# Gate and up products of three feed-forwards in Strassen's seven-product form

## What is computed

```python
h = rms_norm(x, norm_ffn_pre_g[l])
f = (jax.nn.silu(h @ w_gate[l]) * (h @ w_up[l])) @ w_down[l]          # first block
...
def swiglu(h, w_gu, w_down):                                          # second block, twice
    gu = h @ w_gu
    gate, up = jnp.split(gu, 2, axis=-1)
    return (jax.nn.silu(gate) * up) @ w_down
x = x + 0.5 * swiglu(rmsnorm(x, ffn1_norm[l]), ffn1_w_gu[l], ffn1_w_down[l])
```

## Time and profile before

| | us |
|---|---|
| median of 3 runs | 1953.12 (1953.09 to 1955.43) |
| the profiled execution's own time | 1954.23 |
| its span, first to last instruction | 1952.4 |
| PE busy | 1933.2 (99%) |
| DVE busy | 1005.9 (52%) |
| ACT busy | 753.4 (39%) |
| POOL busy | 237.6 (12%) |

### The profile page before, as it was taken

The page is one execution under the profiler, slowest core; times in us unless marked ns, Lnnn a source line. Parts: engine busy times, 40 slices in busy tenths (PEclk is TensorE's granted clock), DMA queues, the critical chain, the costliest instruction groups (busy, mean ns, idle before and its releaser), DMA issues.

```text
span 1952.4 us, 22990 instructions
## 1 busy us (share of the span) xinstructions
PE 1933.2 (99%) x9154; PEld 1576.6 (81%) x9154; DVE 1005.9 (52%) x1525; ACT 753.4 (39%) x1165; POOL 237.6 (12%) x240
## 2 busy tenths in 40 slices
PE   9999999999999999999999999999999999999998
PEld 7777788878888888788888888888887788888887
DVE  6677535373334345633343467887754443334335
ACT  6344534453223234432322356655643343223224
POOL 5210001201011011010100112222010011011010
PEclk9999999999999999999999999999999999999999
DMA  6122133433333323333333232222232233333323
GB/s 175 56 65 65 55 102 103 119 98 97 98 97 97 97 84 110 97 98 97 97 97 98 78 106 65 66 65 65 87 91 61 78 95 97 97 98 97 97 60 103
DMA packets 340763, 176.25 MB, mean 90 GB/s; under 512 B 6481, under 2 KB 339378, under 8 KB 340658
## 3 DMA queue, kind: packets, MB, share of 16 engines
q1 hardware_dynamic: 340658, 174.79, 30.6%
HBM read 172.67 MB, written 2.10 MB: 90 GB/s over the span
## 4 chain that ended last, share of the span: by engine, by line
PE 94%; DVE 3%; ACT 2%; issue 1%; DMA 1%; SPq 0%; POOL 0%; ACTq 0%; DVEq 0%
PE ps L1101 28%; PE ps L1105 28%; PE ps L1103 28%; PE ps L1161 1%; PE ps L1141 1%; PE ps L1150 1%; PE ps L1245 1%; PE ps L1114 1%; PE ps L1263 1%; PE ps L1124 1%; PE ps L1200 1%; PE ps L1131 0%; DVE WL L1555 0%; PE ps L1175 0%; DMA TS<-in_x 0%
## 5 line engine op out<-in xcount | busy, mean ns | idle before, releaser
L1101 PE MATMUL ps<-HH,WH 128*128 128x512 f32 x1728 | 688.3, 398 | 1.1 <-ACT HH L1316 1.1
L1105 PE MATMUL ps<-HL,WH 128*128 128x512 f32 x1728 | 674.1, 390 | 0.8 <-DVE HL L1576 0.8
L1103 PE MATMUL ps<-HH,WL 128*128 128x512 f32 x1728 | 673.6, 390 | 0.8 <-DVE WL L1555 0.8
L1555 DVE TENSOR_TENSOR WL<-RAW,WH 128x1024 fp32r<-128x1024 f32 (+3 forms) x335 | 400.6, 1198 | 530.2 <-ACT WH L1306 530.0
L1306 ACT ACTIVATE WH<-RAW 128x1024 fp32r<-128x1024 f32 (+3 forms) x335 | 337.6, 1010 | 520.9 <-PE ps L1105 517.8
L1101 PEld LDWEIGHTS ps<-HH,WH 128*128 128x128 f32 x1728 | 324.7, 188 | 78.1 <-issue 9.7
L1103 PEld LDWEIGHTS ps<-HH,WL 128*128 128x128 f32 x1728 | 324.9, 188 | 72.6 <-issue 5.5
L1105 PEld LDWEIGHTS ps<-HL,WH 128*128 128x128 f32 x1728 | 324.6, 188 | 71.4 <-DVE HL L1576 2.1
L1101 PE MATMUL ps<-GH,WH 128*128 128x512 f32 x688 | 269.2, 391 | 0.0
L1105 PE MATMUL ps<-GL,WH 128*128 128x512 f32 x688 | 268.0, 389 | 0.0
L1103 PE MATMUL ps<-GH,WL 128*128 128x512 f32 x688 | 267.7, 389 | 0.0
(11 more groups left out here) (203 smaller groups left out, 1555.0 us busy)
## 6 DMA issues: line engine op xcount, KB each, us to landing
RAW<-in_ffn_w_gu SPq DMA_DIRECT2D x88, 512.0 KB, 3.8
RAW<-in_w_in SPq DMA_DIRECT2D x67, 512.0 KB, 3.8
RAW<-in_ffn_w_down SPq DMA_DIRECT2D x32, 512.0 KB, 4.0
RAW<-in_w_gate SPq DMA_DIRECT2D x22, 512.0 KB, 3.7
RAW<-in_w_up SPq DMA_DIRECT2D x22, 512.0 KB, 3.7
RAW<-in_w_out SPq DMA_DIRECT2D x16, 512.0 KB, 4.1
RAW<-in_mem_w_kv SPq DMA_DIRECT2D x16, 512.0 KB, 3.9
RAW<-in_w_down SPq DMA_DIRECT2D x16, 512.0 KB, 3.9
```

What stands on the lines that cost most here:

```text
L1101: e.matmul(bk, wh, xh, start=k == 0, stop=False)
L1103: e.matmul(bk, wl, xh, start=False, stop=False)
L1105: last = e.matmul(bk, wh, xl, start=False, stop=k == kt - 1)
L1555: e.tensor_tensor(at.weight(n, "L"), m["RAW"][:, n % NRAW, 0:kt, :], at.weight(n, "H").bitcast(F32), ALU.subtract).then_inc(*sg.inc("lo", n))
```

## The change

From the fifth tile of the first third on, tiles are no longer made one by one but in pairs of two neighbouring tiles of 128 outputs (`pair`), first the pair's gate, then its up. With the outputs in two halves (tile f and f+1), the 1024 inputs in two halves (chunks 0 to 3 and 4 to 7) and the tokens in two halves (0 to 255 and 256 to 511), the product is a 2 x 2 by 2 x 2 block product, made with seven block products of 128 outputs, 512 inputs and 256 tokens instead of eight (`MIXED`, `product`): 7 x 4 x 3 = 84 matmuls of 256 columns in place of 48 of 512. The first four tiles of each feed-forward (`PLAIN`) stay as they were. Per feed-forward 9 gate pairs and 9 up pairs are made in the new way, 54 in all.

The sums of weights are made by POOL from the raw blocks (`combine_weights`, sums 1 to 4 of 128 x 512, tiles `S`); four of the seven products use a sum, three a half of a raw block. ACT and DVE split each of the seven in parts of 128 x 512 as before. The split places now count in halves, six in all (`HALVES_OF_RING`), so ACT's copy for product j waits for product j-6, and sits in the list behind it and behind the sums that follow it.

The sums of inputs need the normalised input itself: `normal` (DVE, x times gain times R, 8 tiles), `mix` (POOL, four sums of 128 x 256 for each of 4 chunk pairs), `mix_split` (ACT and DVE, into `NH`/`NL`), all during the plain tiles; and `place` (ACT and DVE) writes the normalised input itself over `HH`/`HL` once the last plain product has read them.

The seven results are added with the banks (U for a tile of their sums): ACT copies product 2's bank to U (`sum_one`, `s1`); DVE adds (`sum_one` u2, `sum_two` u3 and c22, `sum_three` c21, `sum_four` c12), each 128 x 256 from PSUM. Products 5 and 6 go on in the banks of products 2 and 1: product 5 (`"a", "21"`) waits for ACT's copy `s1`, and product 6 (`"c", "22"`) for DVE's c22. Silu is then on ACT in three pieces (`corner`, `silu_mixed`), gate by up on DVE (`corner`) and on POOL (`gate_mixed`, one of 128 x 512 and one of 128 x 256), in place of `gate_r` and `gate_up`.

The normalised tiles, `NH` and `NL` lie in memory that the attention's buffers and the masks have at other times, so the level masks and the constants `reset` and `AT` are made on POOL during the down products of the second feed-forward (`LATE`) and no longer at the start. The weight blocks that come by DMA are the same in number and size; of a pair the second comes first, and a raw buffer is free once its splits and sums are done.

The core of the diff:

```diff
+HALVES_OF_RING = 2 * NSPL
+PLAIN = 4
+MIXED = (("b", 2), ("c", 0), ("a", "11"), ("e", 1), ("d", 3), ("a", "21"), ("c", "22"))
...
+    def weigh_pair(self, key, name, c0):
+
+        n, r = len(self.weights), len(self.raws)
+        self.raws += [(name, 0, KD, c0 + P), (name, 0, KD, c0)]
+        self.weights += [("sum", key, 2), ("sum", key, 1), ("half", r + 1, 0), ("sum", key, 3), ("half", r, 1), ("half", r + 1, 1),
+                         ("sum", key, 4)]
+        self.pair_raws[key] = (r + 1, r)
+        self.raw_index += [None] * 7
+        self.needs += [r + 1] * 7
+        self.spent += [r] * 4 + [r + 1] * 2 + [r + 2]
+        self.raw_done[r] = (("lo", n + 4), ("comb", (key, 3)))
+        self.raw_done[r + 1] = (("lo", n + 2), ("lo", n + 5), ("comb", (key, 4)))
+        for _ in range(7):
+            self.offsets.append(self.offsets[-1] + 1)
...
+    def combine_to(self, key, j):
+
+        for i in range(self.combined.get(key, 0) + 1, j + 1):
+            self.tiles.take(("S", key, i))
+            self.step("combine_weights", key, i)
+            self.combined[key] = i
...
+    def ahead(self, n):
+
+        i = self.n_split
+        while i < self.total and self.known.offsets[i + 1] - HALVES_OF_RING <= self.known.offsets[n]:
+            i += 1
+        self.split_to(i)
...
+    def mix(self, gen, c, gcol):
+
+        if c < 4:
+            self.normal(gen, c, gcol)
+            self.normal(gen, c + 4, gcol)
+            for a in range(2):
+                self.tiles.take(("mix", gen, c, a))
+            self.step("mix", gen, c)
+        if c:
+            for a in range(2):
+                self.step("mix_split", gen, c - 1, a, self.mixed_free)
+                self.tiles.give(("mix", gen, c - 1, a), ("op_lo", ("T", gen, c - 1, a)))
+
+    def place(self, gen, c):
+
+        free = (("mm", len(self.weights) - 1),)
+        for a in range(2):
+            self.step("place", gen, c, a, free)
+            self.tiles.give(("N", gen, c + 4 * a), ("op_lo", ("B", gen, c, a)), ("mixed", (gen, c, 3)))
+
+    def pair(self, gen, G, f, up, name, c0, pending):
+
+        key = (G, f, up)
...
+        for i, (b, op) in enumerate(MIXED):
+            if i < 5:
+                self.bank(("pr", key, b))
+            self.step("product", gen, key, i, n + i)
+            if i < 2 and pending:
+                self.split_tile(*pending.pop(0))
+            elif i == 2:
+                self.tiles.take(("u", key))
+                self.step("sum_one", key, n)
+                self.banks.give(("pr", key, "b"), ("part_sum", ("u2", key)))
+            elif i == 3:
+                self.tiles.take(("w", key) if up else tb)
+                self.step("sum_two", key, n)
+                self.banks.give(("pr", key, "e"), ("part_sum", ("u3", key)))
+            elif i == 4:
+                self.step("sum_three", key, n)
+                self.banks.give(("pr", key, "d"), ("part_sum", ("c21", key)))
+                if up:
+                    self.step("gate_mixed", key, 1)
+                    self.tiles.give(("w", key), ("gm", (key, 1)))
+                else:
+                    self.step("silu_mixed", key, 1)
+            elif i == 5:
+                if not up:
+                    self.tiles.take(ta)
+                self.step("corner", key, n)
+                self.banks.give(("pr", key, "a"), ("part_sum" if up else "gate_act", ("c11", key)))
+            elif i == 6:
+                self.step("sum_four", key, n)
+                self.banks.give(("pr", key, "c"), ("part_sum", ("c12", key)))
+                if up:
+                    self.step("gate_mixed", key, 0)
+                    self.tiles.give(("u", key), ("gm", (key, 0)))
+                else:
+                    self.step("silu_mixed", key, 0)
+                    self.tiles.give(("u", key), ("part_sum", ("c12", key)))
+            self.ahead(n + i + 1)
+        return ("mm", n + 6)
...
+                if n or f >= PLAIN:
+                    if f % 2 == 0:
+                        self.pair(gen, G, f, 0, gate, g0 + (f0 + f) * P, pending)
+                        done = self.pair(gen, G, f, 1, up, u0 + (f0 + f) * P, pending)
+                        for a in range(2):
+                            pending.append((("gt", (G, f + a)), ("gm", ((G, f, 1), a)), "G", G, f + a, (("part_sum", ("c11", (G, f, 1))),)))
+                    continue
...
+                if f < PLAIN - 1:
+                    self.mix(gen, f, gcol)
+                else:
+                    self.mix(gen, f, gcol)
+                    self.mix(gen, f + 1, gcol)
+                    for c in range(4):
+                        self.place(gen, c)
+                    self.tiles.give(("R", ("n", gen)), ("N", (gen, 7)), ("gr", key))
+            while pending:
+                self.split_tile(*pending.pop(0))
...
+    def product(gen, key, i, n):
+        b, op = MIXED[i]
+        bk = at.bank(("pr", key, b))[:, 0:256]
+        wh, wl = at.weight(n, "H"), at.weight(n, "L")
+        if i < 5:
+            wait_all(at.bank_free(("pr", key, b)))
+        elif i == 5:
+            g.wait_ge(*sg.at("gate_act", ("s1", key)))
+        else:
+            g.wait_ge(*sg.at("part_sum", ("c22", key)))
+        for c in range(4):
+            ready = ("B" if i in (2, 5, 6) else "T", gen, c, 0 if op in ("11", 0, 1) else 1)
+            xh, xl = at.mixed(op, "H", c), at.mixed(op, "L", c)
+            g.wait_ge(*sg.at("hi", n))
+            g.wait_ge(*sg.at("op_hi", ready))
+            e.matmul(bk, wh[:, c, :], xh, start=i < 5 and c == 0, stop=False, skip_group_check=i >= 5)
+            g.wait_ge(*sg.at("lo", n))
+            e.matmul(bk, wl[:, c, :], xh, start=False, stop=False, skip_group_check=i >= 5)
+            g.wait_ge(*sg.at("op_lo", ready))
+            o = e.matmul(bk, wh[:, c, :], xl, start=False, stop=c == 3, skip_group_check=i >= 5)
+        o.then_inc(*sg.inc("mm", n))
 
...
+        kind, a, b, *_ = plan.weights[n]
+        if kind == "sum":
-            g.wait_ge(*sg.at("mm", n - NSPL))
-        e.activation(at.weight(n, "H"), m["RAW"][:, n % NRAW, 0:kt, :], ACT.Copy).then_inc(*sg.inc("hi", n))
+        else:
+            for i in plan.owners[n]:
+                g.wait_ge(*sg.at("mm", i))
+        e.activation(at.weight(n, "H"), at.raw(n), ACT.Copy).then_inc(*sg.inc("hi", n))
...
+    def sum_one(key, n):
+        g.wait_ge(*sg.at("mm", n + 2))
+        wait_all(at.tile_free(("u", key)))
+        e.activation(at.tile(("u", key))[:, 0:256], at.bank(("pr", key, "a"))[:, 0:256], ACT.Copy).then_inc(*sg.inc("gate_act", ("s1", key)))
...
+    def sum_one(key, n):
+        u = at.tile(("u", key))
+        g.wait_ge(*sg.at("gate_act", ("s1", key)))
+        g.wait_ge(*sg.at("mm", n))
+        e.tensor_tensor(u[:, 256:512], at.bank(("pr", key, "b"))[:, 0:256], u[:, 0:256], ALU.add).then_inc(*sg.inc("part_sum", ("u2", key)))
...
+    def sum_two(key, n):
+        u, home = at.tile(("u", key)), mixed_b(key)
+        g.wait_ge(*sg.at("part_sum", ("u2", key)))
+        g.wait_ge(*sg.at("mm", n + 3))
+        e.tensor_tensor(u[:, 0:256], at.bank(("pr", key, "e"))[:, 0:256], u[:, 256:512], ALU.add).then_inc(*sg.inc("part_sum", ("u3", key)))
+        g.wait_ge(*sg.at("part_sum", ("u3", key)))
+        wait_all(at.tile_free(home))
+        e.tensor_tensor(at.tile(home)[:, 256:512], at.bank(("pr", key, "c"))[:, 0:256], u[:, 0:256], ALU.add).then_inc(
+            *sg.inc("part_sum", ("c22", key)))
...
+    def combine_weights(key, j):
+        ra, rb = plan.pair_raws[key]
+        a, b = m["RAW"][:, ra % NRAW, :, :], m["RAW"][:, rb % NRAW, :, :]
+        out = at.raw_sum(key, j)
+        x, y, op = {1: (b[:, 0:4, :], b[:, 4:8, :], ALU.add), 2: (at.raw_sum(key, 1), a[:, 0:4, :], ALU.subtract),
+                    3: (a[:, 0:4, :], b[:, 0:4, :], ALU.subtract), 4: (a[:, 4:8, :], at.raw_sum(key, 2), ALU.subtract)}[j]
+        g.wait_ge(*sg.at(f"d_raw{rb % NRAW}", rb))
+        g.wait_ge(*sg.at(f"d_raw{ra % NRAW}", ra))
+        if j in (2, 4):
+            g.wait_ge(*sg.at("comb", (key, j // 2)))
+        wait_all(at.tile_free(("S", key, j)))
+        e.tensor_tensor(out, x, y, op).then_inc(*sg.inc("comb", (key, j)))
+
+    def mix(gen, c):
+        a, b = at.tile(("N", gen, c)), at.tile(("N", gen, c + 4))
+        u, v = at.tile(("mix", gen, c, 0)), at.tile(("mix", gen, c, 1))
+        g.wait_ge(*sg.at("N", (gen, c)))
+        g.wait_ge(*sg.at("N", (gen, c + 4)))
+        for i in range(2):
+            wait_all(at.tile_free(("mix", gen, c, i)))
+        e.tensor_tensor(u[:, 0:256], a[:, 256:512], a[:, 0:256], ALU.subtract).then_inc(*sg.inc("mixed", (gen, c, 0)))
+        e.tensor_tensor(u[:, 256:512], b[:, 256:512], a[:, 256:512], ALU.subtract).then_inc(*sg.inc("mixed", (gen, c, 2)))
+        g.wait_ge(*sg.at("mixed", (gen, c, 0)))
+        e.tensor_tensor(v[:, 0:256], b[:, 256:512], u[:, 0:256], ALU.subtract).then_inc(*sg.inc("mixed", (gen, c, 1)))
+        g.wait_ge(*sg.at("mixed", (gen, c, 1)))
```

(9 more changed lines are left out.)

265 lines of the change are left out of this document (199 added, 66 removed).

## The result

| us | before | after |
|---|---|---|
| median of 4 runs each | 1953.11 (1952.75 to 1955.43) | 2111.20 (2109.91 to 2112.27) |
| ratio | | 1.0805, 95% interval 1.0792 to 1.0817 |
| span of the profiled execution | 1952.4 | 2108.7 |

What follows compares the result with a forecast made beforehand. PE was taken as the bound, busy 1933.2 of 1952.4 us. PE's saving, POOL's chain and the starts, -44 + 76 + 24 = +56 us on 1954.2, gave 2010 us, with its own range 1985 to 2040 and an overall range of 1940 to 2050.

Steps and rivals of the forecast that it cites:

- PE's saving, 44 us: PE's matmuls in the new pairs: 10.08 us in place of 10.89, 0.81 saved in each of 54 pairs.
- Rival 4: PE's 256-column matmuls go at half the 512 pace, 0.1134 us each, saving 73 us: 1981 us; chance 0.05.
- The chain on POOL, 18 x 4.2 = 76 us: Gate pairs behind an up pair: POOL's late sums delay `s1` and c22, PE stalls 4.2 us, 18 times.
- DVE and POOL exclude each other: Of two operations with SBUF inputs the second waits for the first; 23.2 us of such work in 20.16 us.
- Rival 2: Gate pairs and starts: POOL's chain without blocking, 18 x 2.5 and 3 x 7.2 us: 1977 us; chance 0.17.
- the walk without blocking: Gate pair behind an up pair, nothing blocking: `s1` 1.6 us late, c22 0.9 more, together 2.5 us.
- The starts, 3 x 8 = 24 us: Where each feed-forward's new form starts, PE waits for the last mixed chunk and `place`: 8 us, three times.
- the other normals, sums and splits of inputs lie beside 43.6 us of plain matmuls: Input preparation during the plain tiles costs nothing; if late, it would add to the start.
- `place` was put at 4.4 us of DVE: At each start, eight `place` pieces on DVE take 0.42 and 0.69 us in turn.
- Rival 3, the clock: After stalls PE gets 1.2 GHz for 3.4 us, costing at most 18 x 1.7 = 31 us: 2041; chance 0.12.
- Rival 1, slack: The POOL chain in gate pairs has slack, stalls small or none: 1910 to 1935 us, up to 1949; chance 0.21.

Runs made afterwards that it cites:

- e16_nosums6: Changed kernel with six plain tiles, `place` by halves, hidden tile's splits later and each weight sum replaced by one fill (values left out): 1934.5 us.
- e1_sum3: Changed kernel with POOL making sum 3 of the next gate pair before the up pair's 512-column `gate_mixed` instead of after it: 2070.3 us.
- e8_nosums: Changed kernel with mixed operands made earlier over the same four plain tiles and each weight sum replaced by one fill (values left out): 1960.4 us.
- e5_fill: Changed kernel with extra, unread 256-column matmuls where PE stands idle, in one PSUM bank kept for them: 2111.7 us.
- e13_banks7: Changed kernel with seven PSUM banks in place of eight and nothing else, the control for e5_fill: 2131.3 us.
- e2_noread: Changed kernel with POOL's weight sums replaced by three fills of similar length that read nothing (values left out), order kept: 2030.7 us.
- e10_plain6: Changed kernel with six plain tiles at each start in place of four, mixed operands made over five, `place` behind the sixth: 2049.6 us.
- e18_between: Changed kernel: six plain tiles, `place` by halves, later hidden-tile splits, gate sums before 512-column `gate_mixed`, up sums 1, 2 between both `gate_mixed`: 1970.1 us.
- e12_later_sum3: Changed kernel with the hidden tile's splits moved behind products 4 and 5, and sum 3 ahead of `gate_mixed`: 2054.5 us.

## Why the prediction was wrong, step by step

- **PE's saving, 44 us: right.** From 600.58 to 601.77 are ten distances of 256-column matmuls, 0.119 us each, the unstalled cycle is 20.16 us, and e16_nosums6 came out within its range (read from PE's distances its pairs lose 4 us and its starts 17: 1954.5 - 39 + 21 = 1936.5, measured 1934.5). Rival 4 is out. So is the figure of the Trainium skill (TensorE: Matmul & The Clock Gate, "Back-to-back issue gap"), 109 ns: the measured 120 decides. PE's busy time rose because matmuls run longer at half speed and beside waits, not by more work.
- **The chain on POOL, 18 x 4.2 = 76 us: right in place, count and wait** (18 waits each for `s1` and c22, 2.64 + 1.64 = 4.28 us, 77 us). e1_sum3 and e8_nosums show it causally. But the pairs lose 118 us. Of the 41 missing, 19 are the clock (e5_fill against e13_banks7). Where the other 22 went, the distances between PE's starts in the trace of the changed kernel show. At each of the 36 waits 0.36 us on average are lost beyond the idle time, 13 in all: a matmul lasts 0.16 us beyond its slot, so the view's idle time starts that much late (597.55 to 600.36 are 2.81 us, which is 2.53 + 0.12 + 0.16), and the next one comes after 0.22 us and not 0.12; at half speed both are more. The matmuls at half speed between the waits lose 29 us, 10 more than the 19: by the difference, that much would have been spent waiting at full speed as well. 77 + 13 + 29 is the 118, to 1 us.
- **DVE and POOL exclude each other: right.** It was said of operations that read SBUF, and e2_noread shows that it is no more than that: POOL's writes alone block nothing. Rival 2, no blocking, is out: e2_noread is nearly that case, 80 us below (2030.7). Its waits for `s1` and c22 are 36.7 us, 2.0 in each of the 18, where the walk without blocking gave 2.5.
- **The starts, 3 x 8 = 24 us: this step failed.** They cost 28 us each, 84 together, and with that 60 of the 101 us missed. The walk began at the last plain matmul with DVE, ACT and POOL free, and "the other normals, sums and splits of inputs lie beside 43.6 us of plain matmuls" was costed at nothing because the busy shares left room. The room was there (in the 20.5 us from 889.0 POOL is busy 13.0, DVE 13.6, ACT 9.7) and useless: the work is a chain that goes back and forth between three queues in order, and each visit holds up what stands behind it. The text said that lateness would add to the start, and gave it no price. e10_plain6, which gives that chain more tiles, one mix in each, takes 16 us off each start. Second, `place` was put at 4.4 us of DVE, and all blocking of a start at up to 2.8 more; its eight pieces take 10.3 us, with six of POOL's sums beside them.
- **Rival 3, the clock: true in kind, smaller in size.** It was given 31 us on top of the forecast's own mechanism, at 18 stalls; it fell at 12, for 6.8 us in place of 3.4, and cost 19. It should have been a term of the sum and not a rival: the forecast itself said that PE would stop 18 times for 4 us, and the earlier trace rows showed what follows such a stop.
- **Rival 1, slack: out.** In no version that makes the sums did the cycle go under 22.1 us.

The sum as measured: -44 + 99 (pairs at full clock) + 19 (clock) + 84 (starts) = 158.

Open is how short a cycle the best order would give: e18_between's trace shows that the exclusion doesn't fill its 22.1 us, but no run made the order shorter with all sums on POOL. Also open is why seven PSUM banks cost 19 us between the second and third feed-forward; the change doesn't touch it.

## What to carry to other kernels

When a transformed product gives other engines its sums, price the sums by walking the queues from the first input on, also through a stretch in which every engine has room: a chain that crosses three in-order queues several times is as long as its visits, whatever the busy shares. A saving of 7% of a pair (0.81 of 10.89 us, 15 us in 18 pairs) does not carry a prologue of 28 us every 18 pairs; count prologues first. And where a forecast has PE stop and go, the lower clock belongs into the sum, but only for stretches in which PE then has work.

## What was not expected of the hardware

- A POOL operation that only writes SBUF leaves DVE's two-input operations alone (690 ns, against 941 beside POOL's sums).
- Two operations that exclude each other overlap at the handover: in turn they took 1.70 us a pair, where 0.61 and 1.25 are their distances alone. A sum of work is too high as a bound by that much for each handover.
- The granted clock stayed at half for 6.8 us behind 12 of 18 stalls of about 4 us in two pieces; in e1_sum3, with one piece of 2 us and one of 0.5, for 3.4 us behind 11 of 18; in e12_later_sum3, with 1.0 and 1.7 us at most, it did not fall in the pairs at all.
- Extra matmuls took away 137 of 196 us at half speed and gave 19 us back: a mean granted clock is no measure of time lost.
